# An encoder layer on one core: waiting tile by tile in the first output and up products, and the norm sums ahead of the last tile

## What is computed

```python
xn = rms_norm(x, g_mix_norm);  z = xn @ w_in
attn = chunk_causal_mla(...)            # 16 heads, from the latent columns of z
rec, h_last = rg_lru(...)               # recurrence over the conv of u
mixed = sigmoid(gate_a) * attn + sigmoid(gate_b) * rec
x = x + mixed @ w_out                   # output projection
up = rms_norm(x, g_ffn_norm) @ w_up     # up projection, 2 * 2816 columns
up_c, ffn_buf_new = causal_dwconv(up, ffn_buf, ffn_conv_w, ffn_conv_b)
gate, val = split(up_c);  x = x + (silu(gate) * val) @ w_down
```

## Time and profile before

| | |
|---|---|
| median of 3 runs | 953.52 us |
| the runs | 949.57 to 953.8 us |
| span of the profiled execution | 950.8 us |
| its own time | not shown on the page; the span lies within the runs |
| TensorE busy | 901.1 us, 95% |
| VectorE busy | 604.5 us, 64% |
| ScalarE busy | 347.4 us, 37% |
| GpSimd busy | 238.3 us, 25% |

### The profile page before, as it was taken

The page is one execution under the profiler, slowest core; times in us unless marked ns, Lnnn a source line. Parts: engine busy times, 40 slices in busy tenths (PEclk is TensorE's granted clock), DMA queues, the critical chain, the costliest instruction groups (busy, mean ns, idle before and its releaser), DMA issues.

```text
span 950.8 us, 18521 instructions
## 1 busy us (share of the span) xinstructions
PE 901.1 (95%) x6689; PEld 849.4 (89%) x6689; DVE 604.5 (64%) x1182; ACT 347.4 (37%) x619; POOL 238.3 (25%) x278
## 2 busy tenths in 40 slices
PE   5999999998799999998989899999999999999997
PEld 5899999987577878776689899999999999999997
DVE  4378634686789888887534487777787777322221
ACT  5341455364343444442423433333333332112111
POOL 4000232462333231231012133333333333201000
PEclk8999999999899999997999999999999999999999
DMA  8333323321000000100002233333322232233321
GB/s 250 81 84 78 95 77 82 84 76 35 15 15 2 14 14 14 47 0 1 1 26 86 67 89 89 88 88 88 88 83 76 84 88 83 84 95 108 102 62 36
DMA packets 114629, 63.53 MB, mean 67 GB/s; under 512 B 7836, under 2 KB 113054, under 8 KB 114588
## 3 DMA queue, kind: packets, MB, share of 16 engines
q1 hardware_dynamic: 112396, 59.17, 22.3%
q0 software_dynamic: 2192, 3.81, 1.6%
HBM read 59.85 MB, written 2.70 MB: 66 GB/s over the span
## 4 chain that ended last, share of the span: by engine, by line
PE 86%; DVE 6%; issue 4%; ACT 2%; POOL 1%; SPq 1%; DMA 0%; DVEq 0%; ACTq 0%; POOLq 0%
PE PS L1141 62%; PE PS L1354 4%; PE PS L1338 4%; PE PS L1319 3%; PE PS L1176 3%; PE PS L1265 2%; PE PS L1308 2%; PE PS L1214 2%; PE PS L1261 1%; PE PS L1292 1%; PE PS L1362 1%; PE PS L1283 1%; DVE small L1010 1%; DMA vrows<-in_state_ffn_conv_dram 0%; PE PS L1325 0%
## 5 line engine op out<-in xcount | busy, mean ns | idle before, releaser
L541 ACT ACTIVATE w_hi<-w_raw 128x1024 fp32r<-128x1024 f32 (+2 forms) x104 | 107.6, 1035 | 373.0 <-PE PS L1141 358.6
L773 DVE TENSOR_TENSOR w_lo<-w_raw,w_hi 128x1024 fp32r<-128x1024 f32 (+2 forms) x104 | 127.3, 1224 | 123.8 <-ACT w_hi L541 123.5
L1141 PE MATMUL PS<-x2h,w_hi 128*128 128x274 f32 x704 | 148.3, 292 | 2.9 <-DVE x2l L1077 2.9
L1141 PE MATMUL PS<-x2l,w_hi 128*128 128x274 f32 x704 | 147.6, 291 | 0.0
L1141 PE MATMUL PS<-x2h,w_lo 128*128 128x274 f32 x704 | 147.5, 291 | 0.0
L1141 PEld LDWEIGHTS PS<-x2h,w_hi 128*128 128x128 f32 x704 | 112.4, 190 | 3.2 <-issue 3.1
L1141 PEld LDWEIGHTS PS<-x2l,w_hi 128*128 128x128 f32 x704 | 112.8, 190 | 0.0
L1141 PEld LDWEIGHTS PS<-x2h,w_lo 128*128 128x128 f32 x704 | 112.0, 190 | 0.0
L1141 PE MATMUL PS<-xnh,w_hi 128*128 128x274 f32 x384 | 83.1, 298 | 4.4 <-DVE w_lo L773 2.3
L1141 PE MATMUL PS<-xnl,w_hi 128*128 128x274 f32 x384 | 81.9, 295 | 0.0
L1141 PE MATMUL PS<-xnh,w_lo 128*128 128x274 f32 x384 | 81.1, 293 | 0.0
(11 more groups left out here) (254 smaller groups left out, 1707.1 us busy)
## 6 DMA issues: line engine op xcount, KB each, us to landing
w_raw<-in_w_up_dram SPq DMA_DIRECT2D x44, 512.0 KB, 3.8
w_raw<-in_w_in_dram SPq DMA_DIRECT2D x24, 512.0 KB, 3.8
w_raw<-in_w_down_dram SPq DMA_DIRECT2D x16, 512.0 KB, 3.7
w_raw<-in_w_out_dram SPq DMA_DIRECT2D x8, 512.0 KB, 3.9
w_raw<-in_w_down_dram SPq DMA_DIRECT2D x8, 384.0 KB, 4.0
xnat<-in_x_prompt_dram SPq DMA_DIRECT2D x4, 512.0 KB, 5.3
w_raw<-in_w_in_dram SPq DMA_DIRECT2D x4, 416.0 KB, 5.6
wq<-in_w_q_b_dram SPq DMA_DIRECT2D x8, 192.0 KB, 2.5
```

What stands on the lines that cost most here:

```text
L541: nc.scalar.activation(hi[:, slot % 2, 0:n], raw[:, slot % 4, 0:n], ACT.Copy).then_inc(s_hi, 1)
L773: tt(lo[:, slot % 2, 0:n], raw[:, slot % 4, 0:n], hi[:, slot % 2, 0:n].bitcast(F32), ALU.subtract).then_inc(s_lo, 1)
L1141: last = mm(PS[:, 2 * rank + j, 0:HT], w[:, slot % 2, cols], x[:, k0 + k, j * HT:(j + 1) * HT], start=(k0 + k == 0 and first), stop=(k0 + ...
```

## The change

Three things in one edit. In `product` the wait for the moving operand moves into the loop over tiles: ahead of tile k it asks for k + 1 tiles instead of for all of the item ahead of the first. The call `midway` stands ahead of the last tile instead of ahead of the fifth; only the first up product has one. The wait for all eight `s_ml` in front of the output projection goes, its first product is given `ready`, and the loop of two turns is written out as eight calls.

```diff
@@ product
                 for t, slot, k0, nk in items:
                     pe.wait_ge(s_lo, t + 1)
-                    if ready is not None:
-                        pe.wait_ge(ready[0], ready[1] + k0 + nk)
                     for k in range(nk):
-                        if midway is not None and k == nk // 2:
+                        if midway is not None and k == nk - 1:
                             midway()
+                        if ready is not None:
+                            pe.wait_ge(ready[0], ready[1] + k0 + k + 1)
                         cols = slice(k * P, (k + 1) * P)
@@ behind the attention
             attend(7, 1)
 
 
-            pe.wait_ge(s_ml, KD)
-            with pe.Fori(0, 2) as it:
-                products(it, G_OUT, mxh, mxl)
+            for r in range(KD):
+                pe.wait_ge(s_free, G_OUT + r - 1)
+                product(mxh, mxl, r % 2, [(I_OUT + r, r, 0, KD)], (s_ml, 0) if r == 0 else None)
             nc.tensor.transpose(PS[0:64, 7, 0:P], st[:, :, :].rearrange("p a b -> p (a b)"), ident[:, :]).then_inc(s_stT, 1)
```

## The result

| | before | changed |
|---|---|---|
| median | 951.35 us (7 runs) | 945.21 us (7 runs) |
| lowest to highest | 949.0 to 953.8 | 942.91 to 946.57 |
| ratio | | 0.9932, 95% interval 0.9917 to 0.9948 |
| span of the profiled execution | 950.8 us | 943.3 us |
| its own time | | 945.21 us, 1.9 more than its span |

The changed kernel is 0.68% faster, by the interval 0.5% to 0.8%. The median of before moved with more runs: the three runs that stood ahead of the prediction gave 953.52 us, all seven 951.35.

A forecast was written before the change was run, and what follows sets the result against it. TensorE, busy 901.1 of 950.8 us, was taken as the bound, so only its gaps and slow stretches could give time back. 2.6 + 0 + 0 + 3.1 = 5.7 us off 953.5 gave 947.8 us, range 945.0 to 951.2.

The forecast's parts named there:

- the clock: First up product: full clock expected once the idle time before it goes, about 1.5 us of the gain.
- the new wait: TensorE ahead of up product 2, for the weight split w_lo: about 1.4 us where before there was none.
- the larger gain: Output projection: 1.2 GHz usually follows its gap too, removal gives 1.5 us more, total 7.2, 946.3 us; chance 0.14.
- Part 1: First output product: waiting tile by tile removes the gap after the attention, 2.6 us, bounds 2.2 to 2.6.
- The 0.33 us ahead of the first matmul: Output projection: time from the end of mxl to the first matmul, with the loop branch, counted within the 2.6 us.
- Part 2: First up product: tile-by-tile waits and sums ahead of the last tile let up product 2 start 3.1 us earlier.
- the sums 2.05 us earlier: First up product: the sum over squares starts at 536.05 instead of 538.11 us, as GpSimd bounds it.
- Both chains: Ahead of the sums: TensorE's tile 6 ends at 535.99 us, GpSimd's eighth addition at 535.78, almost together.
- Rival 1: Up projection: the clock gives nothing back, total gain 4.0 us, 949.5 us; chance 0.24 shared with Rival 2.
- Rival 2: Up product 2: 1.2 GHz follows the new wait, cost 1.5 us, 949.3 us; chance 0.24 shared with Rival 1.
- Rival 3: Output stage: straight code runs out of instructions, 1.2 us lost per product gives 957.4 us; chance 0.04.
- Rival 4: Output or up projection: one part does not do what it says, 950.4 to 950.9 us; chance 0.08.

The follow-up runs named there:

- the loop alone: Before with only the eight output products written out instead of looped: 950.45 us against 951.35, ratio 0.9995.
- each part alone: Changed kernel with only the output projection's edit, 948.80 us, or only the first up product's edit, 948.59 us, against 951.35 of before.

## Why the prediction was right and where it was wrong

**The gain was right; the level was not.** The forecast difference was 5.7 us; the stretch gives 5.8 and 5.7 in two pairs of traces, the medians 6.1. The step that failed is the last of the sum: "so I take the same difference off the median: 953.5 - 5.7 = 947.8". That median was one of three runs that lay 4 us apart, and it stood 2.2 us above the median of seven. Further runs of before beside the experiments bear the lower level out: medians of 951.35 (25 runs), 951.38 (22) and 951.84 us (9). Taken off 951.35, the same difference gives 945.6, against 945.21 measured. The prediction had said that a median of three can lie 1 to 2 us off, but kept 953.5 as its base. The lower end of the range, 945.0, was therefore as good as reached, though the gaps, the clock and the new wait came where the forecast had them. The profiled execution was no better an anchor: most later runs take 1.9 to 2.2 us more than their span (a few up to 2.9), which would put its time at about 952.7 to 953.0, so it too was one of the slower ones.

By its number alone the result would have been taken for the wrong reason. It lies below the forecast's own 946.8 to 948.8 and nearest to "the larger gain (about 946.3)". But that rival's condition, 1.2 GHz behind the gap at the output projection, occurs in none of the six traces that have this gap.

**Where the scatter comes from.** It lies mostly ahead of the change. In the thirteen traces of before, the changed kernel and the experiments the attention ends between 476.09 and 479.41 us, wherever the kernel was changed behind it. One cause can be seen. Between 45 and 46.4 us a wait of TensorE ends (for ScalarE's `nat`), and it lasts 2.09 to 2.10 us in all thirteen. In eight traces 1.2 GHz follows it: the 24 matmuls behind it (four tiles) take 4.7 us, and the attention ends at 478.6 on average. In the other five the clock stays up: the 24 matmuls take 3.15 us, and the attention ends at 476.9. So the fall costs 1.5 us here too, of the 1.7 between the averages. The two traces of before are one of each kind, 1.7 us apart at the attention's end, of which 0.65 lies ahead of this wait. The wait's end and the busy time from 44 to 50 us, first in the trace that the prediction rests on, then in the second:

```profile
45.96 0.56 PE L1141 MATMUL PS<-xnh,w_hi 128*128 128x274 f32 x2 [2.09 <-ACT nat L585]
```
```profile
44.00:50.00 6.00, 4.04 (x20) 4.05 (x21) 4.34 (x20) 5.81 (x18) 0.00 (x0) 0.72 0.35 89
```
```profile
45.31 0.52 PE L1141 MATMUL PS<-xnh,w_hi 128*128 128x274 f32 x2 [2.09 <-ACT nat L585]
```
```profile
44.00:50.00 6.00, 4.69 (x37) 4.70 (x38) 4.88 (x23) 5.78 (x20) 0.00 (x0) 1.00 0.35 93
```

**Part 1** was forecast at 2.6 us and brought 2.65 (gap 2.58 to -0.07), just above its upper bound of 2.6, since the first output matmul starts 0.07 us before the recorded end of the attention. The 0.33 us ahead of the first matmul were to be had as well: 0.28 of them went with the loop alone.

**Part 2** was forecast at 3.1 us and brought 3.2. Its steps: the sums 2.05 us earlier, measured 7.78 - 5.53 = 2.25, for two reasons. Product 0 starts 0.02 us behind the transpose's start and not behind its recorded end, 0.27 us later; and the sums start 0.05 us behind the end of GpSimd's addition, where 0.14 to 0.33 was charged as a handover. Both chains do arrive together: the next pair of matmuls would have started at 532.46, the addition ends at 532.48. From the sums to nrm it took 1.23 us instead of the 1.13 of before, which took 0.1 back, and to the next tile 0.83 us (532.53 to 533.36), not 0.73. The chain behind nrm kept its 7.77 us. The new wait came where it was named, ahead of up product 2 and for w_lo. Its size was put at 1.4 us, counted by starts; so counted it is 1.23, while the profile records 1.07 as idle, less than the 1.2 to 1.6 that the prediction named as a sign of being right.

**The clock.** Forecast: 1.5 us of part 2. The kernel with 22 filling matmuls confirms it by 1.4 to 1.5 without shortening the gap.

**The rivals.** Rival 1 let the clock's part be chance. It isn't at this place: in all five traces that have the gap of 2.87 us with nothing in it, 1.2 GHz follows, and in none of the six traces with a gap at the output projection (2.3 to 3.1 us). In these traces the outcome goes with the place and not with the gap's length; what it is about the place wasn't found. In the first 50 us the chance is there, as the traces above show. Rival 2 did not come: full clock follows the wait of 1.07 us, and the one of 1.83 us with the sums behind the last tile. Rival 3 fell with the written-out loop alone (49.12 against 49.11 us). Rival 4 fell with each part alone.

**The chances.** The 0.66 for a gain of over 0.5% came true narrowly: 5.8 us are 0.6% of the time, and the interval ends at 0.5%. That the medians show 6.1 and not 5.8 is luck. The 0.50 for 946.8 to 948.8 did not come, and that by the base alone. The scatter of the first 480 us belongs in the level's range.

## What to carry to other kernels

Where one product waits for a whole operand, ask which tile is really late: if only the last is, waiting tile by tile hides everything up to it, and a sum that stands in the middle of the product has to move with it, or its own producer becomes the stall. Then follow the chain behind the sum to the next product that needs its engine's queue; here it was a weight split that stood behind a chain it did not depend on, and moving it into an idle stretch took the new wait away. And set a forecast as a difference on the stage that the change touches; put the level's scatter into the range separately.

## What the runs showed of the hardware

The low clock behind idle time can't be read off the gap's length: gaps of 2.18 us (one trace) and 2.87 us (all five) were followed by 1.2 GHz, gaps of 2.3 to 2.6 us (all five) and 3.05 us (one) at another place of the same program by 2.4 GHz. A third gap, of 2.09 us in all thirteen traces, at about 46 us, went both ways: 1.2 GHz in eight, 2.4 GHz in five. The Trainium skill, "TensorE: Matmul & The Clock Gate", section "What's actually happening", says that the gate's watching runs freely and isn't tied to the kernel's start, so that the point of change varies from run to run. The gap at 46 us agrees with that, eight to five. Behind the gap of 2.87 us the low clock came each time, but its start varied: over the first 0.84 us of matmuls the granted clock is 1.00 in three traces, 0.87 in one and 0.54 in one. Whether it came did not vary there, nor at the output projection.

A fall of the clock had the same price at both places where it could be measured against its absence, in a dense stream of these matmuls: 1.5 us behind the wait at 46 us (4.7 against 3.15 us for 24 matmuls), 1.4 to 1.5 us behind the gap at the up projection.

Matmuls that nobody reads, put into a gap, made the stretch 1.4 to 1.5 us shorter, since they kept the clock up.

The recorded idle time ahead of a matmul understates what a wait costs in this stream: 1.07 us recorded were 1.23 us by the starts, and taking the wait away gave 1.3 us.
